# The first difference of a weight pair in SBUF, its low part on GpSimd

## The reference

```python
h2 = rmsnorm(x, norm_mlp)
return x + jnp.square(jax.nn.relu(h2 @ w_up)) @ w_down
```

## Time and profile before

| | us |
|---|---|
| median of 3 runs (lowest, highest) | 2443.09 (2443.07, 2443.64) |
| profiled execution, its own time | 2443.72 |
| its span in the trace | 2441.7 |
| PE busy | 2427.5 (99%) |
| DVE busy | 1358.2 (56%) |
| ACT busy | 951.0 (39%) |
| POOL busy | 1373.3 (56%) |

### The profile page before, as it was taken

How to read it: one execution, slowest core, us unless ns; L and a number is a source line. 1 busy time by engine, 2 the same in 40 slices (tenths; PEclk the granted TensorE clock), 3 DMA queues, 4 the chain that set the end, 5 groups by cost and what they waited for, 6 DMA issues and landing times.

```text
span 2441.7 us, 34615 instructions
## 1 busy us (share of the span) xinstructions
PE 2427.5 (99%) x12088; PEld 2020.3 (83%) x12088; DVE 1358.2 (56%) x1942; ACT 951.0 (39%) x1363; POOL 1373.3 (56%) x1682
## 2 busy tenths in 40 slices
PE   9999999999999999999999999999999999999999
PEld 7888888888998888888888889988777777888887
DVE  7884412358666768944123565638866665723323
ACT  5331232242543523312322425424577776422222
POOL 6556655556666755566555566657332334555554
PEclk9999999999999999999999999999999999999999
DMA  5222223242423422222222324353211112232322
GB/s 191 85 70 94 95 97 101 95 147 70 172 106 120 173 95 86 70 95 95 98 100 95 146 69 173 114 197 103 68 50 42 61 42 70 92 103 93 102 92 93
DMA packets 64909, 247.75 MB, mean 101 GB/s; under 512 B 7200, under 2 KB 9888, under 8 KB 63520
## 3 DMA queue, kind: packets, MB, share of 16 engines
q1 hardware_dynamic: 62496, 218.13, 26.5%
q10 hardware_dynamic: 2304, 28.17, 2.9%
HBM read 244.17 MB, written 2.10 MB: 101 GB/s over the span
## 4 chain that ended last, share of the span: by engine, by line
PE 88%; DVE 4%; ACT 4%; issue 2%; DVEq 1%; POOL 1%; DMA 0%; ACTq 0%; SPq 0%; POOLq 0%
PE ps L704 83%; ACT set_hi L1408 1%; PE ps L1080 1%; PE ps L1093 1%; DVEq L2275 1%; PE ps L1109 1%; DVE set_lo L2288 1%; DVE ps L2281 1%; PE ps L1048 1%; POOL w_lo L601 1%; DVE set_lo_f L2281 1%; ACT A_hi L1441 1%; ACT prob L1719 0%; PE ps L1113 0%; DMA w_raw<-weights 0%
## 5 line engine op out<-in xcount | busy, mean ns | idle before, releaser
L601 POOL TENSOR_TENSOR w_lo<-w_raw,w_hi 128x256 fp32r<-128x256 f32 x1448 | 1180.6, 848 | 875.7 <-ACT w_hi L1329 646.1
L704 PE MATMUL ps<-H_hi,w_hi 128*128 128x512 f32 x1616 | 641.9, 397 | 0.2 <-DVE H_lo L2477 0.2
L704 PE MATMUL ps<-H_hi,w_lo 128*128 128x512 f32 x1616 | 629.4, 389 | 0.0
L704 PE MATMUL ps<-H_lo,w_hi 128*128 128x512 f32 x1616 | 629.1, 389 | 0.0
L1329 ACT ACTIVATE w_hi<-w_raw 128x1024 fp32r<-128x1024 f32 x295 | 310.0, 1054 | 481.8 <-PE ps L704 481.1
L704 PEld LDWEIGHTS ps<-H_hi,w_hi 128*128 128x128 f32 x1616 | 303.4, 188 | 69.5 <-issue 9.0
L704 PEld LDWEIGHTS ps<-H_lo,w_hi 128*128 128x128 f32 x1616 | 303.5, 188 | 64.8 <-issue 4.5
L704 PEld LDWEIGHTS ps<-H_hi,w_lo 128*128 128x128 f32 x1616 | 303.3, 188 | 63.9
L704 PE MATMUL ps<-A_lo,w_hi 128*128 128x512 f32 x744 | 289.5, 389 | 0.0
L704 PE MATMUL ps<-A_hi,w_hi 128*128 128x512 f32 x688 | 267.8, 389 | 0.0
L704 PE MATMUL ps<-A_hi,w_lo 128*128 128x512 f32 x688 | 267.7, 389 | 0.0
(11 more groups left out here) (331 smaller groups left out, 4028.7 us busy)
## 6 DMA issues: line engine op xcount, KB each, us to landing
w_raw<-weights SPq DMA_DIRECT2D x403, 512.0 KB, 3.3
mod_w<-mod_weights ACTq DMA_DIRECT2D x8, 3072.0 KB, 11.3
toeplitz<-biases SPq DMA_DIRECT2D x14, 128.0 KB, 2.1
out<-X SPq DMA_DIRECT2D x7, 256.0 KB, 2.0
X<-x SPq DMA_DIRECT2D x3, 512.0 KB, 8.3
decay_sb<-decay ACTq DMA_DIRECT2D x1, 1024.0 KB, 7.1
ctx_sb<-context ACTq DMA_DIRECT2D x1, 1024.0 KB, 14.7
X<-x SPq DMA_DIRECT2D x2, 256.0 KB, 3.9
```

The lines of the kernel that those rows point to most:

```text
L601: last = nc.gpsimd.tensor_tensor(lo[:, c:c + LOW_COLS], w_raw[:, q, c:c + LOW_COLS], hi[:, c:c + LOW_COLS].bitcast(F32), ALU.subtract)
L704: mm = nc.tensor.matmul(dst, w[l], xs[r], start=start and a == 0, stop=stop and a == 2, skip_group_check=joined)
```

## The change

The S3 sum of the later pairs goes to SBUF as S1 does, in place 1 of `set_lo_f`. So DVE now waits, ahead of the S3 sum, until PE has used the S3 of the pair before (`free_of`), because its low part lies in the same bytes. The S2 sum reads S3 from SBUF. DVE's S3 low part in the loop is gone; POOL makes it, behind A11 low and ahead of A22 low, with a wait for the S2 sum (which reads S3 before it is written over) and for ACT's high part.

```diff
@@ sum_place @@
-            if FAST_JOBS[n][2] == 0 or piece == "S1":
+            if FAST_JOBS[n][2] == 0 or piece in ("S1", "S3"):
                 return set_lo_f[:, place(piece, PAIR_OF[n]), :]
             return ps[:, SUM_OF_BANK[piece], :]
@@ POOL, piece_lows @@
                 if piece == "S2":
                     pool.wait_ge(piece_summed["S4"], i + 1)
+                if piece == "S3":
+                    pool.wait_ge(piece_summed["S2"], i + 1)
@@ POOL, the loop over pairs @@
                         if j + 1 < DT // 2:
                             piece_lows("A11", m + 2)
+                            piece_lows("S3", m + 2)
                         if j:
                             piece_lows("A22", m)
@@ DVE, fast_up @@
                         if more:
-                            sum_low("S3", n + 2)
                             sum_of("S2", n + 2)
                             sum_low("S2", n + 2)
```

## The result

The changed kernel took 2448.1 us in the median of 13 runs (2447.02 to 2449.58), the kernel before 2443.43 in 13 runs (2442.92 to 2444.39). The ratio is 1.0020 with a 95% interval of 1.0012 to 1.0028: 4.7 us slower, a small loss but clear of the noise. The forecast was 2.1 us slower. The profiled execution took 2447.92 us, its span is 2445.7 us against 2441.7.

A forecast was written before the change was run, and what follows sets the result against it. TensorE, busy 99% of the span, was taken as the bound. The 0.65 us won at A11(2) is lost to a later load, and 0.42 more: 5 groups x 0.42 = +2.1 us, 2445.2 us, range 2441.0 to 2448.3.

The forecast's parts named there:

- the path: Fast up-projection groups: first chain earlier, A11(2) wait gone, pair 3 load issued 0.62 us later, A11(3) 0.42 us later.
- PE waits for S3 low: Rival at pair 1 of a group: S3 low at most 0.1 us late, costing 0.5 us in all; chance 0.02.
- nothing moves: Rival: ACT also binds the S2 high part for k = 2, A11(2) waits as before, 2443.1 to 2445; chance 0.04.
- the gap at A11(2): PE's wait ahead of A11(2), pair 2 of each fast group: forecast to go, 0.65 us per group.
- The rival of the covered load: POOL's 1.18 us lead swallows the two S3 operations; at best 3.2 us gained, 2439.9 us; chance 0.24.
- GpSimd as the bound: Rival: DVE stretches POOL by 2.15 instead of 1.10, A11(3) 1.47 us later, 2450.4 us; over 4.9 us slower, chance 0.12.
- From issue to the S3(3) sum are 4.66 us: Pair 3 load to DVE's sum: the old interval was kept, so the sum comes at 628.12 us.
- If the S3(3) sum is itself stretched ... I take 0: DVE's S3(3) sum: stretching could add up to 0.37 us; the forecast counted none.
- The 0.42 us per group: Net lateness of A11(3) in each fast group: forecast at 634.18 us, for 5 groups +2.1 us.
- The likeliest case: The forecast's own sum, over the whole kernel: 0.5 to 4.9 us slower; chance 0.58.
- the range that was named: Forecast time of the whole kernel: 2441.0 to 2448.3 us.

The follow-up runs named there:

- e7: Kernel before the change, with the load of pair 3 also waiting for ACT's high part of S4(2), no arithmetic changed; 2448.41 us, ratio 1.0021.
- e4: Kernel before the change, with GpSimd forming A11 low of later pairs twice, first into an unread scratch place; 2453.48 us, ratio 1.0041.

## Why the prediction was right and wrong

**Right: the path.** The chain came step by step, all in us of group 1 (forecast times counted from 605.69). ACT's high part of S1(1) was forecast at 10.28 and came at 10.46, the squares at 13.03 and 13.46, the S2(2) high part at 14.34 and 14.78. ACT's timeline after:

```profile
615.79 0.63 ACT L1411 ACTIVATE set_hi<-set_lo_f 128x512 fp32r<-128x512 f32 x1 [1.13 <-DVE set_lo_f L2284]
...
618.79 0.63 ACT L1443 ACTIVATE A_lo_f<-E 128x512 f32<-128x512 f32 x1 [0.53 <-DVE E L2311]
...
620.11 0.59 ACT L1411 ACTIVATE set_hi<-ps 128x512 fp32r<-128x512 f32 x1
```

`second_of` waited for PE as said, at 617.12 with 0.21 us idle, and its E began at 12.31 (forecast 12.29). The load was forecast at 17.77 and went out at 17.98, the S3(3) sum at 22.43 and came at 22.62, A11(3) at 28.49 and came at 28.57. POOL's timeline, with S3 low at 620.47 between A11 and A22 low:

```profile
616.50 1.70 POOL L624 TENSOR_TENSOR set_lo<-set_lo_f,set_hi 128x256 fp32r<-128x256 f32 x2
618.16 2.34 POOL L624 TENSOR_TENSOR set_lo<-w_raw,set_hi 128x256 fp32r<-128x256 f32 x2
620.47 1.43 POOL L624 TENSOR_TENSOR set_lo<-set_lo_f,set_hi 128x256 fp32r<-128x256 f32 x2
621.86 1.43 POOL L624 TENSOR_TENSOR set_lo<-w_raw,set_hi 128x256 fp32r<-128x256 f32 x2
...
627.32 1.93 POOL L624 TENSOR_TENSOR set_lo<-set_lo_f,set_hi 128x256 fp32r<-128x256 f32 x2 [1.29 <-ACT set_hi L1411]
```

From 616.50 to 621.86 + 1.43 = 623.29 these eight took 6.79 us; the forecast was 6.75. That the sum fits so well is partly luck: against the 1.43 of other pairs the S1 pair was longer by 0.27 us, where 0.70 was forecast for the S3 sum and E beside it, and the A11 pair by 0.91, where 0.40 was forecast for S2(2). The rivals that PE waits for S3 low and that nothing moves fall: PE had no wait at S3, and the gap at A11(2) shrank. The rival of the covered load falls with the 1.38 us idle time of the S3(3) sum. GpSimd as the bound did not come as described: A22 low was not stretched beyond the forecast.

**Half right: the gap at A11(2).** It went in groups 4 and 5; in groups 1 to 3 some 0.28 us of 0.65 stayed. (In group 5 there had been only 0.40 us to win; the forecast took the 0.65 of group 1 for all five.) I let POOL pay for an encounter with DVE and DVE pay only 0.2 us at S2(1); E took 1.11 instead of 0.71 and S2(1) 1.06 instead of the 0.90 I took. It cost nothing in the end, since all of this gain is given back at A11(3).

**Wrong: what follows the issue of the load.** The failed step is "From issue to the S3(3) sum are 4.66 us", taken as a constant, with "If the S3(3) sum is itself stretched ... I take 0". The 0.42 us per group are the sum of four terms; the two profiles of the changed kernel give them in ten groups, each against the same group before:

| per group, us | forecast | measured, mean of ten | from, to |
|---|---|---|---|
| the load is issued later | +0.62 | +0.75 | +0.46 to +0.84 |
| issue to start of the S3(3) sum | 0 | +0.22 | -0.10 to +1.07 |
| the S3(3) sum itself | 0 | +0.18 | -0.01 to +0.57 |
| end of that sum to A11(3) | -0.20 | -0.22 | -0.35 to -0.06 |
| A11(3) | +0.42 | +0.93 | +0.11 to +1.81 |

5 x 0.93 = 4.7 us, the measured difference. The two terms set to nothing carry 0.40 of the missing 0.51 us. Most of the rest is in the first term: with S2(1) at 1.06 us instead of 0.90, ACT's S1(1) high part and POOL behind it came 0.18 us later in group 1 than forecast. Landing of the second block, in the page's view of DMA for groups 1 and 2 (the last number is us from issue to landing; the last row is the queue of instructions in the 6.5 us after the issue in group 2):

```profile
w_raw<-weights SPq DMA_DIRECT2D x1, 512.0 KB, 4.1
...
w_raw<-weights SPq DMA_DIRECT2D x1, 512.0 KB, 5.4
...
q8 instruction: 1, 0.02, 0.9%
```

The one group that I had read does not show this tail, but the trace of before did: the second block of an earlier load of its group 2, issued at 695.55, took 5.4 us as well:

```profile
w_raw<-weights SPq DMA_DIRECT2D x1, 512.0 KB, 5.4
```

And a slow landing now goes to PE in full: in group 2 of the changed kernel the block took 1.26 us longer to land than in group 1, and A11(3) came 1.32 us later. Before, the sum had waited only 0.15 to 0.50 us for its block, with next to no loss at A11(3). Whether the landings also make the wider spread, 2.6 us of 13 runs against 1.5, is not shown: in e7 the load is as late, and its 11 runs spread over 1.2 us.

The length of the S3(3) sum turns on a tenth of a microsecond. In group 1 the S3(3) sum at 627.95 began just before the second of POOL's two operations from 627.32; it took 0.69 us, and POOL's pair 1.93 instead of the 1.43 of other pairs. In group 3 the block had landed 0.13 us later, and POOL's operation was under way; the sum took 1.22 and POOL's pair 1.43:

```profile
801.87 1.43 POOL L624 TENSOR_TENSOR set_lo<-set_lo_f,set_hi 128x256 fp32r<-128x256 f32 x2 [1.29 <-ACT set_hi L1411]
```

The Trainium skill, "SBUF — State Buffer", section "Who interferes with whom", says that whichever of the two begins first keeps the other out. The trace agrees on who pays; what the second pays here is 0.50 and 0.52 us, where the other had 0.64 and 0.66 us of its record still to run. In the forecast I had weighed this rule for POOL alone and given DVE nothing to pay at this sum.

**The chances.** The likeliest case, 0.5 to 4.9 us slower, is the one that came, near its upper end; its own sum was less than half of it. That 2448.1 us lies inside the range that was named, 0.2 us from its end, is owed to the width of the range and not to the sum.

## What to carry to other kernels

When work moves to an in-order queue, look not only for who waits for that work, but for what it is put ahead of: here two subtractions of 0.7 us stood ahead of the one that lets a load start, and moving one line behind it turned 4.7 us of loss into a version no slower than before. A load that is late by less than its slack costs nothing: before the change DVE already waited 0.15 to 0.50 us for it, and PE hardly felt it. Once PE, at the end of the chain behind it, waits too, the cost is the lateness plus the tail of the landing times, so that tail has to be read over all groups and added to the sum. A gain ahead of a wait is kept only if the next wait moves as well.

## What the runs showed of the hardware

The second of the two 512 KB blocks that SP loads for pair 3 landed in 4.0 to 4.3 us in 31 of the 40 groups of eight profiles, and in 4.4 to 6.3 us in nine. In each of these nine a packet or two of an instruction queue (8 or 14) fell in the 6.5 us after the issue; in eight other groups such a packet was there and the landing took 4.0 to 4.3 us. The seventeen with a packet are groups 2 and 5 of every profile and group 1 of e4. That code loading delays the load is an inference from this; no run moved it.

When an instruction of DVE with two SBUF inputs and a low part of POOL meet, the one that begins later pays, and what it pays follows what the other has left to run. In the five groups of the eight profiles such a DVE instruction (0.69 us alone, E 0.71) took a median 1.06 us when POOL's had 0.40 to 0.55 us left (143 cases) and 1.13 with 0.55 to 0.70 left (33 cases). A low part on POOL (0.74 us alone) took 1.19 when DVE's had 0.55 to 0.70 us left (291 cases) and stayed at 0.74 with under 0.20 left (131 cases).
